# Output products of four heads side by side in block 1's attention

## The reference

```python
h = rms_norm(x, norm_mix_pre[i])
z = h @ w_in[i]
c_q, c_kv, k_rope, q_c, k_c, v_c, g_a, g_b, g_c = jnp.split(z, split_points, axis=-1)
o_a = mla_attention(...)      # 8 heads: softmax(q k^T) v, 64 columns of values each
o_b = fourier_mix(h)          # Fourier transform over tokens and groups of features
o_c = windowed_gqa(...)       # 8 heads, 2 groups of keys and values, a sink in the softmax
merged = (sigmoid(g_a) * (o_a @ w_branch_a[i]) + sigmoid(g_b) * (o_b @ w_branch_b[i])
          + sigmoid(g_c) * (o_c @ w_branch_c[i]))
```

## Time and profile before

| | |
|---|---|
| time, median of 3 runs | 1862.18 us (1862.01 to 1862.36) |
| the profiled execution | 1862.04 us |
| its span, first to last instruction | 1860.2 us |
| busy: PE, PEld | 99%, 83% |
| busy: DVE, ACT, POOL | 65%, 53%, 8% |
| granted clock of PE, mean | 0.999 |
| matmuls recorded | 9632 |
| matmuls recorded for block 1's head outputs (L906) | 8 per pair of heads, 64 per layer |
| heads of layer 0 | about 56.6 to 142.3 us of the span |
| heads of layer 1 | about 493.5 to 579.2 us |

### The profile page before, as it was taken

The page is one execution under the profiler, slowest core; times in us unless marked ns, Lnnn a source line. Parts: engine busy times, 40 slices in busy tenths (PEclk is TensorE's granted clock), DMA queues, the critical chain, the costliest instruction groups (busy, mean ns, idle before and its releaser), DMA issues.

```text
span 1860.2 us, 27281 instructions
## 1 busy us (share of the span) xinstructions
PE 1848.5 (99%) x9632; PEld 1547.1 (83%) x9632; DVE 1208.9 (65%) x1493; ACT 991.0 (53%) x1299; POOL 156.6 (8%) x260
## 2 busy tenths in 40 slices
PE   9999999999999999999999999999999999999998
PEld 7878888887877888888888887788888888778887
DVE  6875666658876666657756646666666556576555
ACT  5774454446675454445544557544454445575443
POOL 7110010002210010000100021000010000100000
PEclk9999999999999999999999999999999999999999
DMA  7345556554445465556566454465565565535553
GB/s 228 115 160 187 181 204 203 179 184 158 150 136 176 169 226 188 178 187 203 187 203 202 160 193 158 154 202 176 186 204 181 182 202 188 186 114 168 185 189 113
DMA packets 204985, 332.17 MB, mean 179 GB/s; under 512 B 11488, under 2 KB 150368, under 8 KB 204896
## 3 DMA queue, kind: packets, MB, share of 16 engines
q1 hardware_dynamic: 200240, 319.08, 51.3%
q0 software_dynamic: 3120, 11.02, 1.7%
q10 hardware_dynamic: 1536, 0.95, 0.2%
HBM read 329.96 MB, written 1.05 MB: 178 GB/s over the span
## 4 chain that ended last, share of the span: by engine, by line
PE 95%; DVE 1%; POOL 1%; issue 1%; DMA 1%; ACT 0%; ACTq 0%; DVEq 0%; POOLq 0%
PE ps L767 21%; PE ps L607 19%; PE ps L590 18%; PE ps L599 18%; PE ps L785 11%; PE ps L643 3%; PE ps L878 2%; PE ps L890 2%; PE ps L906 2%; DMA freq<-freq_dram 0%; POOL hid L2903 0%; DVE wlo L1973 0%; DVE eb L2438 0%; DMA gains<-gains_dram 0%; DVE wlo L1967 0%
## 5 line engine op out<-in xcount | busy, mean ns | idle before, releaser
L1967 DVE TENSOR_TENSOR wlo<-raw,whi 128x2048 fp32r<-128x2048 f32 (+1 forms) x294 | 664.1, 2259 | 178.6 <-ACT whi L1432 175.2
L1432 ACT ACTIVATE whi<-raw 128x2048 fp32r<-128x2048 f32 (+3 forms) x306 | 569.5, 1862 | 130.1 <-PE ps L599 130.1
L767 PE MATMUL ps<-act,whi 128*128 128x512 f32 x1728 | 403.6, 390 | 0.0
L767 PEld LDWEIGHTS ps<-act,whi 128*128 128x128 f32 x1728 | 323.5, 188 | 66.6
L1495 ACT ACTIVATE hid<-ps 128x512 f32<-128x512 f32 x54 | 32.2, 597 | 396.2 <-PE ps L785 396.2
L2039 DVE TENSOR_TENSOR hid<-ps,hid 128x512 f32<-128x512 f32 x54 | 37.4, 692 | 314.2 <-ACT hid L1495 314.2
L785 PEld LDWEIGHTS ps<-act,wlo 128*128 128x128 f32 x1728 | 214.5, 192 | 4.2
L785 PE MATMUL ps<-act,wlo 128*128 128x256 f32 x1728 | 215.8, 283 | 0.0
L590 PE MATMUL ps<-wlo,act 128*128 128x512 f32 (+2 forms) x768 | 207.4, 385 | 0.4 <-DVE wlo L1967 0.4
L607 PE MATMUL ps<-whi,act 128*128 128x512 f32 (+2 forms) x768 | 204.7, 386 | 1.1 <-DVE wlo L1967 0.6
L599 PE MATMUL ps<-whi,act 128*128 128x512 f32 (+2 forms) x768 | 200.9, 382 | 0.6 <-DVE act L1973 0.6
(11 more groups left out here) (261 smaller groups left out, 1952.4 us busy)
## 6 DMA issues: line engine op xcount, KB each, us to landing
raw<-ffn_w_gate_dram SPq DMA_DIRECT2D x88, 512.0 KB, 4.0
raw<-ffn_w_up_dram SPq DMA_DIRECT2D x88, 512.0 KB, 4.9
raw<-ffn_w_down_dram SPq DMA_DIRECT2D x88, 512.0 KB, 4.3
raw<-w_in_dram SPq DMA_DIRECT2D x64, 512.0 KB, 4.5
raw<-w_ffn_gate_dram SPq DMA_DIRECT2D x44, 512.0 KB, 4.0
raw<-w_ffn_up_dram SPq DMA_DIRECT2D x44, 512.0 KB, 4.9
raw<-w_ffn_down_dram SPq DMA_DIRECT2D x44, 512.0 KB, 4.2
raw<-a_w_qkv_dram SPq DMA_DIRECT2D x24, 512.0 KB, 4.5
```

The lines of the kernel that those rows point to most:

```text
L767: nc.tensor.matmul(ps[:, 2 * g + j, :], vh[:, k, g, j * P:(j + 1) * P], both[:, 4 * half + k, :, :], start=half == 0 and k == 0, stop=False)
L1432: nc.scalar.activation(whi[:, u % SLOTS, half:words], raw[:, u % SLOTS, half:words], ACT.Copy)\
L1967: nc.vector.tensor_tensor(wlo[:, u % SLOTS, 0:words], raw[:, u % SLOTS, 0:words], whi[:, u % SLOTS, 0:words].bitcast(F32), ALU.subtract)\
```

## The change

A table `OUTPUTS_AT` says which pairs of heads are multiplied with their values in which step: pairs 0 and 1 in step 4, 2 and 3 in step 8, 4 and 5 in step 12, pair 6 in step 14, and pair 7, as before, inside GATE_A. In steps 2, 6 and 10 there are no output products any more; in steps 4, 8 and 12 those of two pairs stand one behind the other. `outputs` takes any even number of heads, waits for the banks and the turned probabilities of all of them first, and counts `pair_done` behind each pair. Up to four heads' turned probabilities live at once, so a second buffer `probT_more` is added, at the address of `hid_hi` and `hid_lo`; heads with sc % 4 of 2 or 3 use it. ACT's and DVE's reads of the pairs (`pair_hi`, `pair_lo`) move to the same steps. Block 2's attention is not touched.

```diff
@@ -117,6 +117,7 @@
 }
 
 PROBS = 3
+OUTPUTS_AT = {4: (0, 1), 8: (2, 3), 12: (4, 5), 14: (6,), 16: (7,)}
 WARM_SHORT, WARM_LONG, WARM_START = 6, 3, 18
 AHEAD_ONE, AHEAD_TWO = 6, 3
 
@@ -275,6 +276,7 @@
         act_hi, act_lo = both[:, :, 0, :], both[:, :, 1, :]
         gains = sb("gains", [P, 2, D])
         hid = sb("hid", [P, T, CH])
+        probT_more = under("probT_more", [P, 2, T, S])
         hid_hi = sb("hid_hi", [P, CH // P, S], F32R)
         hid_lo = sb("hid_lo", [P, CH // P, S], F32R)
         prob = sb("prob", [P, PROBS, T, S])
@@ -365,6 +367,12 @@
 
             two = buf[:, t, :].rearrange("p (a n) -> p a n", a=2)
             return two[:, :, fa_place(g):fa_place(g) + P + 1]
+
+        def probs_place(sc, causal):
+
+            if causal:
+                return probT[:, sc % 2]
+            return probT[:, sc % 4] if sc % 4 < 2 else probT_more[:, sc % 4 - 2]
 
         def scale_places(w):
 
@@ -903,7 +911,7 @@
                 def output(kt):
                     c0 = kt * P if causal else 0
                     o = ps[VD * odd:VD * (odd + 1), 3 if causal else 5 + 2 * (pair % 2), c0:S]
-                    return nc.tensor.matmul(o, v[:, kt], probT[:, sc % 2, kt, c0:S],
+                    return nc.tensor.matmul(o, v[:, kt], probs_place(sc, causal)[:, kt, c0:S],
                                             start=kt == 0, stop=kt == T - 1)
 
                 return Head(score_bank, score, turn_probs, output_bank, output)
@@ -918,14 +926,15 @@
                         if t == T - 1:
                             last.then_inc(sem("score_done"), 1)
 
-            def outputs(even, odd):
-
-                even.output_bank()
-                odd.output_bank()
-                for kt in range(T):
-                    even.output(kt)
-                    last = odd.output(kt)
-                last.then_inc(sem("pair_done"), 1)
+            def outputs(*some):
+
+                for one in some:
+                    one.output_bank()
+                for even, odd in zip(some[0::2], some[1::2]):
+                    for kt in range(T):
+                        even.output(kt)
+                        last = odd.output(kt)
+                    last.then_inc(sem("pair_done"), 1)
 
             def attend(heads, values, others):
 
@@ -957,8 +966,8 @@
                         scores(heads[s + 1])
                     elif s % 2 and s + 2 < n:
                         scores(heads[s + 1], heads[s + 2])
-                    if s >= 2 and s % 2 == 0:
-                        outputs(heads[s - 2], heads[s - 1])
+                    if s in OUTPUTS_AT:
+                        outputs(*heads[2 * OUTPUTS_AT[s][0]:2 * OUTPUTS_AT[s][-1] + 2])
                     if s == 0:
                         beside_first()
                     heads[s].turn()
@@ -1555,11 +1564,11 @@
                 act.wait_ge(sem("turn_done"), w.at("turn_done", tn + 1))
                 bank = ps[:, 2 if causal else 2 + tn % 2, :].rearrange("p (k n) -> p k n", k=T)
                 if causal:
-                    nc.scalar.activation(probT[:, sc % 2, 0, :], bank[:, 0, :], ACT.Copy)
-                    nc.scalar.activation(probT[:, sc % 2, 1, P:S], bank[:, 1, P:S], ACT.Copy)\
+                    nc.scalar.activation(probs_place(sc, True)[:, 0, :], bank[:, 0, :], ACT.Copy)
+                    nc.scalar.activation(probs_place(sc, True)[:, 1, P:S], bank[:, 1, P:S], ACT.Copy)\
                         .then_inc(sem("turn_read_a"), 1)
                 else:
-                    nc.scalar.activation(probT[:, sc % 2, :, :], bank, ACT.Copy).then_inc(sem("turn_read_a"), 1)
+                    nc.scalar.activation(probs_place(sc, False), bank, ACT.Copy).then_inc(sem("turn_read_a"), 1)
 
             def pair_hi(pair, dst):
                 act.wait_ge(sem("pair_done"), w.at("pair_done", pair + 1))
@@ -1683,8 +1692,7 @@
                     if s % 2:
                         probs_turned(s, TN_HEAD + s, False)
                     head_exps(s + 1)
-                    if s >= 1 and s % 2 == 0:
-                        pair = (s - 1) // 2
+                    for pair in OUTPUTS_AT.get(s, ()):
                         pair_hi(pair, (co_hi if pair < H1 // 2 else oc_hi)[:, pair % (H1 // 2), :])
                     if s < heads:
                         if s == 0:
```

## The result

The kernel with the change takes 1864.76 us (median of 22 runs, 1864.31 to 1866.06), the kernel before 1862.07 us (22 runs, 1861.82 to 1862.40): 2.7 us more, a ratio of 1.0015 with a 95% interval of 1.0009 to 1.0021. That is slower by less than 0.2%. The span of the profiled execution is 1862.9 us against 1860.2.

A forecast was written before the change was run, and what follows sets the result against it. PE's own instruction stream was taken to set the time. Per layer -0.89 us net saving + 0.71 + 1.15 us of waits = +0.97, +1.94 for two layers, on the 1862.18 us median: 1864.1 us, range 1861.6 to 1865.7.

The forecast's parts named there:

- rival C: Second two heads of each doubled group cost 1.01 us, not 0.86; 1865.0 us, or 1865.6 with another delay; chance 0.14.
- The removal of a group: Output groups behind heads 2, 6 and 10 disappear from PE's stream, saving 1.15 + 1.15 + 1.17 = 3.47 us per layer.
- The doubled group: Behind heads 4, 8 and 12, four more matmul pairs add 0.86 us each, 2.58 us per layer.
- Head 2's turn: Waits for DVE's normalised probabilities once its output group is gone; costs 0.71 us, leaving 0.44 of the 1.15 saved.
- Head 3's turn: Would start at 70.34 with probabilities usable at 70.29: no wait, but only 0.05 us of room.
- The second tile of `half_job(0)`: Behind head 6, waits until DVE has read over_tokens(3)'s bank; 1.15 us, all that the removal there saved.
- The rest has room: Other operands, such as the probabilities of heads 6, 10 and 14, are ready in time; no further wait, no cost.
- A: Neither wait appears because DVE and ACT run ahead; only the net saving, 1860.4 us; chance 0.06.
- B: Only one wait appears: 1861.8 us with head 2's alone, 1862.7 with the bank's alone; chance 0.14.
- D: Idle time behind head 6 lowers PE's granted clock from 2.4 to 1.2 GHz; 1878 us; chance 0.01.
- E: PE's stream held the groups apart for another reason, so no effect; 1862.2 us; chance 0.05 including smaller shifts.
- estimate of 0.11 us: Two tiling-mode drains per output group, from the skill's 128 cycles; would make the total saving 0.6 us instead of 1.8.

The follow-up runs named there:

- e6: Kernel before with only pairs 0 and 1 grouped (step 4) and DVE reading over_tokens(1)'s bank once instead of twice; 1863.27 us, 1.05 more than before.
- e4: Kernel before with only pairs 3 and 4 grouped in step 10 and pairs 5 and 6 in step 14; 1861.03 us, ratio 0.9995.
- e3: Kernel before with only pairs 2 and 3 grouped, in step 8; 1863.82 us, ratio 1.0008.

## Why the prediction was right, and where it was short

The forecast was 1864.1 us, an increase of 1.94 us; measured are 1864.76 us and an increase of 2.69. The time alone would not have told the forecast from rival C (1865.0 us), which lies nearer to it; the rows do. Step by step:

- *The removal of a group*, 1.15 or 1.17 us per step: measured 1.16 in steps 6 and 10.
- *The doubled group*, for which 0.86 us was taken out of a range from 0.86 to 1.01: measured 0.85, 0.86 and 0.86. Rival C is out.
- *Head 2's turn*: its start 1.58 us behind head 3's scores, and 0.44 us left of the saving: measured 1.58 and 0.42.
- *Head 3's turn* with 0.05 us of room: no wait (69.85 to 70.71 is 0.86).
- *The second tile of `half_job(0)`*: the wait takes all that the removal gives: measured -1.16 and +1.18. The price was right, but its parts were not, and that they made up for each other was luck. I took the 0.18 us between DVE's end and the tile's start for the delay of the wait and called the room nil. The delay is 0.05 us (85.85 to 85.90), so the room was 0.13, and the hole is 1.05 instead of 1.15; but the first pass after it takes 0.13 us longer, a term that the prediction did not have.
- *"The rest has room"* is the step that failed. For step 3 it followed the probabilities of head 3 and left out `over_width(2)`, though its second tile waits in `free_before` for the bank that `over_tokens(1)` left. DVE's two subtractions stand behind head 3's maxima in its order and end at 68.93 in before, at 68.98 in after, the same but for the later start of the trace. Before, the tile came at 69.19, 0.26 us behind them, and 0.05 of that is the delay of such a wait; brought 0.42 us nearer, it found the bank taken for 0.21 us. With 0.11 for its slower first pass that costs 0.31 us per layer, and e6 took 0.23 to 0.29 of it away. Twice 0.31 is 0.6 of the 0.75 us by which the increase was under-forecast (1.94 against 2.69); the rest is spread over the terms.

Rivals A and B are out by the two waits, each present in both layers. D is out: the granted clock is 0.999 as before, and 1.00 from 80 to 94 us, the stretch with the hole of 1.05 us. E is out by the lengths of the groups.

A merged group saves 0.30 us in the rows of after, 1.16 less 0.86. The Trainium skill, TensorEngine Tiling (Array Packing), section Key Properties, says that a change of tiling mode drains TensorE; a cost at the ends of a group agrees with that in kind, but no run shows how much of the 0.30 us is a drain. The prediction's estimate of 0.11 us, from the 128 cycles of the Trainium skill, TensorE: Matmul & The Clock Gate, section Step-by-step, would have been about a third of it.

## What to carry to other kernels

On an engine that is always busy, work that looks movable at no cost may be the cover of somebody's wait: an output group left out brought every later operand 1.15 us nearer, and three of them were not there yet. Before moving such a block, list for each instruction behind it every wait that it stands on, the release of the buffer that it writes as well as its inputs, and compare each with the new start; the order inside the other engines' programs decides, not their busy share. Here the same grouping is worth 0.25 us per place and layer where probabilities and banks are early (groups in steps 10 and 14, e4: the stretch of the heads is 0.5 us shorter in both layers, the median 1.0 us lower, which the ratio's interval alone does not tell from no change), and costs 0.7 to 0.9 where they are just in time (groups in steps 4, 6 and 8).

## What the runs showed of the hardware

A product that waited for its bank is slower at its start than one in the stream: its first pass takes 1.05 us instead of 0.92 for four matmuls of 512 columns (85.90 to 86.95), and 0.35 instead of 0.24 for two of 258 (69.03 to 69.38). So each of these holes costs 0.11 to 0.13 us more than its length. In the kernel before, the weight load of the same product starts 0.12 to 0.13 us ahead of it (69.07 and 69.19; 85.12 and 85.25), in after at the same moment (69.03; 85.90). That would account for it, but no run tested it. The hole before head 2's turn adds only 0.02: to the product behind it are 0.38 us (67.64 to 68.02) instead of 0.36.

From the end of DVE's last reading to the product that waits for the bank are 0.05 to 0.06 us (85.85 to 85.90; 68.98 to 69.03; 85.27 to 85.33 in e3), but from the end of a normalisation to the turn that waits for it 0.14 to 0.15 us (63.95 to 64.09; 67.49 to 67.64). One delay cannot stand for the other; why they differ, no run shows.

A short hole of PE, 0.21 us, is not in PE's list of waits at all, since the matmuls before it are counted as busy almost to its end (68.97 of 69.03). The starts of successive groups show it, and so does the list of the weight loads.
